# Weights of the i and f gates: two products on two banks, or one padded product on one bank

## What is computed

```python
p = h @ w_in[layer] + b_in[layer]
u_s5, q, k, v, o_pre, i_pre, f_pre, g_s5, g_m = _split_columns(p)   # i_pre, f_pre: 4 columns each
...
log_i = to_chunks(i_pre, -jnp.inf)
log_f = to_chunks(jax.nn.log_sigmoid(f_pre.astype(f32)), 0.0)
```

## Time and profile before

| | |
|---|---|
| median of 3 runs | 1368.21 us (1365.33 to 1369.11) |
| profiled execution | 1367.95 us, of it the span 1366.2 us |
| PE busy | 1222.2 us (89%) |
| DVE / POOL / ACT busy | 866.4 / 521.8 / 425.4 us |
| granted TensorE clock, mean | 0.99 |
| packets under 512 B | 10380 of 130794 |

### The profile page before, as it was taken

The page is one execution under the profiler, slowest core; times in us unless marked ns, Lnnn a source line. Parts: engine busy times, 40 slices in busy tenths (PEclk is TensorE's granted clock), DMA queues, the critical chain, the costliest instruction groups (busy, mean ns, idle before and its releaser), DMA issues.

```text
span 1366.2 us, 14256 instructions
## 1 busy us (share of the span) xinstructions
PE 1222.2 (89%) x4539; PEld 642.2 (47%) x4539; DVE 866.4 (63%) x1726; ACT 425.4 (31%) x1126; POOL 521.8 (38%) x578
## 2 busy tenths in 40 slices
PE   7999979999877877877898777899999999999997
PEld 2676545565322222323443222564444445999443
DVE  2446478575575766777667578568997443677335
ACT  2212244333443343443434434322115111222000
POOL 1000057665777776777777777001111000000000
PEclk9999999999999999999999999999999999999999
DMA  9797599999999999999999999363333344354440
GB/s 346 294 328 278 171 334 398 406 406 404 405 409 410 409 409 409 392 409 409 409 409 407 408 406 404 145 246 123 124 123 124 107 157 166 140 183 146 169 181 31
DMA packets 130794, 397.32 MB, mean 291 GB/s; under 512 B 10380, under 2 KB 11788, under 8 KB 130463
## 3 DMA queue, kind: packets, MB, share of 16 engines
q0 software_dynamic: 74448, 271.09, 50.3%
q1 hardware_dynamic: 54404, 120.14, 24.4%
q10 hardware_dynamic: 1868, 5.18, 1.0%
HBM read 395.32 MB, written 1.05 MB: 290 GB/s over the span
## 4 chain that ended last, share of the span: by engine, by line
PE 46%; DMA 22%; POOL 12%; DVE 10%; issue 5%; DVEq 3%; ACT 1%; POOLq 0%; ACTq 0%
PE psum L673 18%; DMA gathered<-in_peer_u_dram,expert_idx 16%; PE psum L1270 6%; PE psum L1309 6%; POOL gathered L582 6%; POOL gathered L596 6%; PE psum L985 6%; DMA gathered<-in_peer_v_dram,expert_idx 3%; DVE work L1771 3%; DMA weight_ring<-in_w_in_dram 2%; DVE gathered L2116 2%; DVE work L2405 2%; PE psum L781 2%; PE psum L700 1%; PE psum L755 1%
## 5 line engine op out<-in xcount | busy, mean ns | idle before, releaser
L985 PE MATMUL psum<-gathered,modr 128*128 128x512 f32 x1024 | 500.1, 618 | 115.1 <-DMA gathered<-in_peer_v_dram,expert_idx 96.9
L2116 DVE CUSTOM_DVE_ANT_0 gathered<-gathered,psum 128x1024 f32<-128x1024 f32 x256 | 312.2, 1220 | 181.4 <-DMA gathered<-in_peer_u_dram,expert_idx 180.0
L985 PEld LDWEIGHTS psum<-gathered,modr 128*128 128x128 f32 x1024 | 180.0, 192 | 412.9 <-DMA gathered<-in_peer_v_dram,expert_idx 245.9
L582 POOL DMA_INDIRECT gathered<-in_peer_u_dram,expert_idx x256 | 249.0, 972 | 265.1 <-DVE expert_idx L1779 167.4
L596 POOL DMA_INDIRECT gathered<-in_peer_v_dram,expert_idx x256 | 243.8, 952 | 92.5 <-issue 70.8
L673 PE MATMUL psum<-weight_ring,featT 128*128 128x512 f32 x384 | 172.2, 603 | 1.7 <-ACT featT L1361 1.7
L1524 ACT ACTIVATE gel<-dots 128x1 f32<-128x1 f32 x256 | 51.6, 201 | 285.6 <-DVEq L2118 285.4
L1771 DVE TENSOR_TENSOR work<-work 128x1088 f32<-128x1088 f32 (+4 forms) x107 | 99.9, 951 | 26.8 <-ACT work L1624 18.7
L673 PEld LDWEIGHTS psum<-weight_ring,featT 128*128 128x128 f32 x384 | 71.7, 191 | 92.2 <-issue 90.0
L673 PE MATMUL psum<-featT,weight_ring 128*128 128x128 f32 (+2 forms) x768 | 107.6, 296 | 3.6 <-ACT featT L1361 1.5
L673 PEld LDWEIGHTS psum<-featT,weight_ring 128*128 128x128 f32 x768 | 100.6, 191 | 19.2 <-issue 11.5
(11 more groups left out here) (365 smaller groups left out, 1370.0 us busy)
## 6 DMA issues: line engine op xcount, KB each, us to landing
weight_ring<-in_w_in_dram SPq DMA_DIRECT2D x13, 2048.0 KB, 9.1
weight_ring<-in_ada_w_dram SPq DMA_DIRECT2D x10, 2048.0 KB, 17.5
weight_ring<-in_w_up_dram SPq DMA_DIRECT2D x8, 2048.0 KB, 8.3
weight_ring<-in_w_down_dram SPq DMA_DIRECT2D x8, 2048.0 KB, 7.7
weight_ring<-in_peer_wq_dram SPq DMA_DIRECT2D x3, 2048.0 KB, 12.7
gathered<-in_ada_w_dram SPq DMA_DIRECT2D x2, 2048.0 KB, 14.6
gathered<-in_w_in_dram SPq DMA_DIRECT2D x2, 2048.0 KB, 13.4
gathered<-in_peer_u_dram,expert_idx POOLq DMA_INDIRECT x256, 11.0
```

Source lines behind the costliest of these rows:

```text
L582: pool.indirect_dma_start(u_rows[:, slot, :], None, T["peer_u"], bass.IndirectOffsetOnAxis(ap=expert_idx[:, r % 2, k:k + 1], axis=0),).the ...
L985: mm = pe.matmul(psum[:, SUM_BANK + half, :], diag[:, e % 8, :], v_rows[:, slot, 512 * half:512 * (half + 1)], start=(e % EXPERTS == 0), s ...
L2116: dve.tensor_tensor_reduce(u_rows[:, slot, :], u_rows[:, slot, :], h2_rows[t], 1.0, 0.0, ALU.mult, ALU.add, dots[:, col:col + 1])
```

## The change

The weights of both gates are kept in one block of 36 columns: i in columns 0 to 3, zeros in 4 to 31, f in 32 to 35. POOL writes the zeros at the start, in one memset placed in front of the iota. Two loads in place of one bring the weights, each with 8 separate pieces of 16 B per partition. PE makes one product of 36 columns per feature block, 8 in place of 16, into one bank and as one turn, so every later turn uses the other of the two banks. ACT reads both parts from that bank and counts one turn read.

```diff
-        w_if = sb("w_if", [P, KD, 2 * MH])
+        w_if = sb("w_if", [P, KD, 32 + MH])
...
-        turns += [("h0", 1, q) for q in range(2)] + [("if", c, 0) for c in range(2)]
+        turns += [("h0", 1, q) for q in range(2)] + [("if", 0, 0)]
...
             pool.memset(quarter_rows[:, :], 0.0)
+            pool.memset(w_if[:, :, MH:32], 0.0).then_inc(flag("if_padded"), 1)
...
-            pe.wait_ge(flag("in_if"), 32)
-            banks = [begin_turn("if", c, 0) for c in range(2)]
+            pe.wait_ge(flag("in_if"), 48)
+            pe.wait_ge(flag("if_padded"), 1)
+            bank = begin_turn("if", 0, 0)
             for k in range(KD):
-                for c in range(2):
-                    last = pe.matmul(banks[c][32 * c:32 * c + MH, 0:LEN], w_if[:, k, MH * c:MH * (c + 1)],
-                                     featT[:, k, :], start=(k == 0), stop=(k == KD - 1))
-                    if k == KD - 1:
-                        last.then_inc(turned, 1)
+                last = pe.matmul(bank[0:32 + MH, 0:LEN], w_if[:, k, :], featT[:, k, :], start=(k == 0),
+                                 stop=(k == KD - 1))
+            last.then_inc(turned, 1)
...
-            load(w_if[:, :, :], T["w_if"], "in_if")
+            for c in range(2):
+                load(w_if[:, :, 32 * c:32 * c + MH], T["w_if"][:, :, MH * c:MH * (c + 1)], "in_if")
             load(b_if[:, :], T["b_if"], "in_if")
...
-            act.wait_ge(flag("in_if"), 32)
-            for c in range(2):
-                read_turn(row_a[:, c, :], turn_bank("if", c, 0)[32 * c:32 * c + MH, 0:LEN], "if", c, 0,
-                          func=ACT.Identity, bias=b_if[:, c:c + 1])
+            act.wait_ge(flag("in_if"), 48)
+            turn_wait(act, "if", 0, 0)
+            act.activation(row_a[:, 0, :], turn_bank("if", 0, 0)[0:MH, 0:LEN], ACT.Identity, bias=b_if[:, 0:1])
+            act.activation(row_a[:, 1, :], turn_bank("if", 0, 0)[32:32 + MH, 0:LEN], ACT.Identity,
+                           bias=b_if[:, 1:2]).then_inc(turn_read, 1)
...
-            turn_read_wait(act, "if", 1, 0)
+            turn_read_wait(act, "if", 0, 0)
```

## The result

The changed kernel takes 1381.36 us (median of 5 runs, 1380.3 to 1383.53) against 1368.21 before. The ratio is 1.0105, with a 95% interval of 1.0094 to 1.0116. (The ratios in this document are those on record, which come from all the runs that were taken side by side; they differ from the quotient of the two medians, here 1.0096, by up to 0.0009.) The forecast was 1373.0 with a range up to 1377.2. Its direction was right, though its chances put slower (0.48) no higher than no change (0.49); its size was not: the loss is 13.2 us where 4.8 were forecast. The profiled execution took 1380.3 us, 1378.6 of it the span: 12.4 more than the span before.

What follows compares the result with a forecast made beforehand. The prediction took PE to carry the chain (46%), with PE's list and the cu chunk's transfer ending almost together near 78 us. Stall +5.3, memset +0.22 and turn -0.77 gave +4.75, so 1373.0 us, range 1367.0 to 1377.2.

Steps and rivals of the forecast that it cites:

- The place and the chain: At 54 to 79 us: ACT's last issue stands, its copies end at 64.6, PE's cc group starts 5.6 us late.
- The turn: At the gates, 907 to 933 us: PE's wait for ACT's reading of the first gate turn goes, -0.77 us.
- The products: At the gates: eight 36 column products are 16 records at 0.23 us, so halving the count brings nothing.
- The small pieces: DMA engines, 65 to 79 us: 0 to 63 ns per piece, 0 to 6.3 us on the cu landing, covered, taken as 0.
- part 3 (b): ACT's queue near 57 us: 168 pieces per engine against room for 150 to 154, so a stall, +5.3 us.
- the forecast's upper bound: ACT's queue only 128 pieces deep: the issue ends near 68.5 us, +10.1, and the time is about 1377.8 us.
- lower end, no stall: ACT's queue near 57 us: no stall at all, 0 us.
- The memset: At POOL's start, before PE's first product at 7.50 us: +0.22 us, bounds 0 and 0.25.
- ACT's queue takes everything: Rival at ACT, 57.5 us: no stall, -0.55 to +0.45 us, 1367.7 to 1368.7 us; chance 0.30.
- The product as two in a row: Rival at 910 us: a 36 column product takes the time of two, +3.7 us, 1376.7 or 1371.9; chance 0.03.

Runs made afterwards that it cites:

- the kernel with the small loads first: Changed kernel with b_if and log_dt issued ahead of the two w_if loads: 1377.58 us, ratio 1.0077 to the kernel before.
- the one with the small pieces first: Changed kernel with the two w_if loads first in ACT's group, ahead of ada_b: 1437.05 us, ratio 1.0023 to the kernel before, in the slower series.

## Why the prediction was wrong

*What held.* The place and the chain: ACT's issues stand, the copies at L1388 come late, PE's cc group waits for them, the cu chunk has landed by then, and all behind it moves. The turn: -0.77 forecast, -0.76 measured. The products: one record of 36 columns costs what a pair side by side costs. The small pieces cost nothing where they are covered.

*The step that failed* is part 3 (b), the room in ACT's queue, where the forecast says that SP stands "until about 150 to 154 are left" and lets ACT's last issue end when 14 to 18 pieces per engine have started, at 63.7 us. It counted the pieces of the waiting DMA itself. Each of SP's chunks has 64 of its own, so 154, 153 and 150 are just as well 90, 89 and 86 *ahead* of it. With chunks of one size the two readings cannot be told apart; on ACT, where a load of 64 per engine is followed by one of a quarter of a piece, they come out far apart. The pieces of ACT's queue that had started in the changed kernel, from 54 us to 65.2 and to 70.6, where the two issues end:

```profile
q10 hardware_dynamic: 442, 2.99, 74.0%
...
q10 hardware_dynamic: 995, 3.94, 65.1%
```

Ahead of the second `w_if` load are 4 x 8 + 64 = 96 per engine; 442/16 = 27.6 had started, so it ends with 68 ahead. Ahead of `b_if` are 160; 995/16 = 62.2 had started, so it ends with 98 ahead. In the kernel with the small loads first the second `w_if` load ends with 104 - 31.4 = 73 ahead. By the forecast's reading, with the own pieces in, the second load would have ended when 160 - 154 = 6 pieces had started, before 61.0 (8.3 had then), and `b_if` with it. What all runs fit is: an issue goes in at once with 64 pieces per engine or fewer unstarted ahead of it, stands with 96 or more, and ends when 65 to 98 of them are left; a waiting DMA of a quarter of a piece stands as one of 64 does. It is no single number. ACT's second `w_if` issues ended with 67 to 73 ahead, its `b_if` issues with 90 to 98, and SP's issues, 86 to 90 in the kernel before, ended with 65 in the one with the small pieces first (1007 started by 71.18). What sets it stays open.

By SP's 86 to 90, read so, the rows of before would have pointed to the larger loss: `b_if` must wait until 160 - 90 = 70 pieces per engine have started, which is past 69.4 us, where 45.6 had the earlier trace rows. That is at least the forecast's upper bound of +10.1 in place of +5.3. The forecast gave its lower end, no stall, a chance of 0.30, and its upper end none: the 1377.8 us that it names for it lie outside its range, which ends at 1377.2.

*What was missing.* A second cost that hangs on the first: the forecast had no term for it. The sum moved PE's list as a block, 5.6 us later, at unchanged durations. A wait of 13.37 us of PE brings the clock down, and the cc group pays 2.84 us more; the filler products show it by leaving the wait and taking the clock's fall away. The sum in the forecast's way, by what was measured: +13.11 for the wait, +2.84 for the clock, -0.35 for the wait of the chunk that goes, and -0.76 for the turn are +14.8, where L1109 starts 14.40 us later. The memset took 0.35 where 0.22 was forecast (back to 7.49 where it is moved), but at 54 us nothing of it can be seen. The profiled spans differ by 12.4, since some 2 us come back on the way to 1100 us, 1.7 of them where the low clock near 1070 us is missing after; the medians differ by 13.2.

*The rivals.* That ACT's queue takes everything fell: two issues stand. The page "DMA: Bandwidth & Descriptors" of the Trainium skill (Anatomy of one DMA) says that many descriptors can be emitted before the cost shows, and says it of the DMAs that GpSimd issues; the prediction carried it over to ACT. On ACT's queue it does not hold without a limit: at 2 x 64 pieces per engine behind 32 others the second `w_if` issue and that of `b_if` cost 14 us, while the same two loads took 1.33 us with nothing ahead of them. The product as two in a row fell too.

## What to carry to other kernels

A load that is cut into many small pieces is paid for by the engine that issues it, and by whatever stands behind it in that engine's list: count the pieces of the DMAs ahead, and keep even the tiniest DMA from standing behind many pieces if the engine has work that somebody waits for. Put such loads where their issuer is idle, or load contiguously and rearrange on an idle engine. To put them ahead of the slow large ones took the stand away here too, but only while the other queue was almost empty, and the chunk landed later. And where a change makes PE wait, look at the granted clock behind the wait: after 8.84 and 13.37 us it was down and the next 32 records took 1.9 and 2.8 us more; after 1.28 us it was not.

## What was unexpected of the hardware

- A DMA of four 8 B pieces took 5.45 us to issue, behind 128 small pieces per engine; in front of them 0.40 us.
- A piece of 16 B took at most 12 ns of a DMA engine with no large ones beside it. Beside another queue's 2 KB pieces the two queues went one for one, and a small piece got its turn every 93 ns.
- With PE idle for 13.4 us the granted clock fell to half, and the 32 records that followed took 10.01 us; with filler products in the wait they took 7.14.
- The kernel before ran 4.9% longer in one series than in another (1433.43 against 1366.83 us), on a chip of the same number, with a mean granted clock of 0.96 to 0.97 against 0.99.
